# Second mixer of a diffusion backbone: input rows on all 128 partitions, copies divided anew between two engines, and the last modulation unit computed among the gated products

## The reference, cut to what matters

```python
h  = modulate(rms_norm(x, norm1_g[layer]), sh1, sc1)          # latent, 512 tokens
hc = modulate(rms_norm(ctx, norm1_g[layer]), sh1c, sc1c)      # context, 256 tokens
# s5_mixer: 64 groups of 16 channels, 64 complex states per group, two directions
for di, rev in enumerate((False, True)):
    ...
    yc_d, h_ctx = s5_scan(u_c, lam_bar, b_bar, c_mat, h0, rev, need_ctx)     # only h_ctx is used
    yl_d, _ = s5_scan(u, lam_bar, b_bar, c_mat, h_ctx, rev, True)
    y = y + yl_d
def glu(t):
    z = gelu(t)
    val, gt = jnp.split(z @ glu_w + glu_b, 2, axis=-1)
    return val * sigmoid(gt)
x = x + g1 * glu(y)
```

## Time and profile before

| | |
|---|---|
| median of 3 runs | 2510.58 us (2507.99 to 2512.06) |
| the profiled execution | 2506.16 us |
| its span | 2504.4 us, so 1.8 us lie around it |
| the mixer in it | from 1461.3 to 1760.7 us |
| busy | PE 86%, DVE 44%, ACT 20%, POOL 17% |
| mean granted PE clock | 0.952 |

### The profile page before, as it was taken

One profiled execution on the slowest core, in us unless ns is written; L12 is line 12 of the kernel. 1 busy time (PEld: TensorE's weight loads), 2 busy tenths in 40 slices (PEclk: granted clock), 3 DMA queues, 4 the chain that ended last, 5 costly groups with the idle time before them and its releaser, 6 DMA issues. The chain is left out here.

```text
span 2504.4 us, 40476 instructions
## 1 busy us (share of the span) xinstructions
PE 2143.6 (86%) x11989; PEld 1189.9 (48%) x11990; DVE 1092.3 (44%) x2311; ACT 509.8 (20%) x945; POOL 433.9 (17%) x359
## 2 busy tenths in 40 slices
PE   5889999997999999999999816699789999988874
PEld 3765444744544444444444405354444444444442
DVE  8853365944543333333333338942532222222222
ACT  3443233611121111111111125220221111100000
POOL 1000000002012222222222210000122222232332
PEclk9999999998999999999999968799799999999997
DMA  9971002003799999999999669830499999899996
GB/s 358 386 265 46 34 34 84 1 1 131 264 346 355 354 358 357 359 351 350 355 358 358 202 158 329 275 146 0 160 404 375 361 363 358 274 390 372 385 385 207
DMA packets 173622, 666.72 MB, mean 266 GB/s; under 512 B 37666, under 2 KB 48898, under 8 KB 129882
## 3 DMA queue, kind: packets, MB, share of 16 engines
q1 hardware_dynamic: 121410, 564.71, 58.7%
q0 software_dynamic: 36160, 64.84, 11.0%
q10 hardware_dynamic: 15960, 35.96, 4.1%
HBM read 617.29 MB, written 86.09 MB: 281 GB/s over the span
## 5 line engine op out<-in xcount | busy, mean ns | idle before, releaser
L1518 PE MATMUL banks_l<-slotw_l,xTw_l 128*128 128x512 f32 x800 | 358.2, 601 | 27.7 <-issue 27.7
L1529 PE MATMUL banks_l<-slotn_l,xTn_l 128*64 128x256 f32 x2816 | 325.0, 383 | 34.5 <-issue 34.5
L1529 PEld LDWEIGHTS banks_l<-slotn_l,xTn_l 128*64 128x64 f32 x2816 | 212.0, 137 | 178.9 <-issue 104.8
L1518 PEld LDWEIGHTS banks_l<-slotw_l,xTw_l 128*128 128x128 f32 x800 | 148.5, 191 | 239.3 <-issue 239.3
L1568 PE MATMUL banks_l<-slotn_l,late_l 128*64 128x512 f32 x704 | 189.9, 615 | 19.6 <-DVE late_l L1356 17.9
L1547 PE MATMUL banks_l<-slotw_l,late_l 128*128 128x512 f32 x400 | 191.8, 602 | 15.4 <-DVE late_l L1338 15.4
L977 POOL DMA_INDIRECT xgw_l<-moe_h,idxw_l x58 | 60.6, 1045 | 741.0 <-PE banks_l L1463 367.1
L1005 POOL DMA_INDIRECT moe_acc<-late_l,idxn_l x88 | 151.2, 1718 | 190.5 <-DMA moe_acc<-late_l,idxn_l 172.5
L937 POOL IOTA slotw_l<- 128x1 f32 x2 | 0.3, 140 | 729.1 <-POOLq L69 431.3
L1335 DVE TENSOR_TENSOR late_l<-late_l,banks_l 128x256 f32<-128x256 f32 x50 | 21.0, 421 | 240.2 <-ACT late_l L1107 240.2
L556 PE MATMUL ps_a<-W_a,hT_a 128*128 128x512 f32 x288 | 124.9, 595 | 0.0
(11 more groups left out here) (433 smaller groups left out, 3235.0 us busy)
## 6 DMA issues: line engine op xcount, KB each, us to landing
slotn_l<-in_exp_w_gate SPq DMA_DIRECT2D x88, 1024.0 KB
slotn_l<-in_exp_w_up SPq DMA_DIRECT2D x88, 1024.0 KB
slotn_l<-in_exp_w_down SPq DMA_DIRECT2D x88, 1024.0 KB, 12.1
slotw_l<-in_exp_w_gate SPq DMA_DIRECT2D x50, 1024.0 KB
slotw_l<-in_exp_w_up SPq DMA_DIRECT2D x50, 1024.0 KB
slotw_l<-in_exp_w_down SPq DMA_DIRECT2D x50, 1024.0 KB
w_p<-in_mod_w SPq DMA_DIRECT2D x12, 2048.0 KB, 15.4
W_a<-in_ar_w_in SPq DMA_DIRECT2D x5, 2048.0 KB, 9.4
```

Of the source, the lines that this page charges most:

```text
L1518: last = pe.matmul(pGU_w, xT_w[b % 2][:, k, :], wgu[0][b % WIDE_RING][:, :, k, :], start=(k == 0), stop=(k == KD - 1))
L1529: last = pe.matmul(pGU_n[H * side:H * side + H, b % 2], xT_n[b % 2][:, k % 4, H * (k // 4):H * (k // 4) + H], w[:, :, k, P * side:P * side ...
```

## The change

The input is laid out on all 128 partitions. Latent rows go straight into `x[:, 0:4]` (`XL`), two halves of four steps with 64 chunks each; context rows (`XC`) go four by 32, two steps each. There are six adds, six squares and six scalings where there were eight, and the eight copies to `x` are gone. ACT's queue starts with `vec`. `s5_r` is loaded by SP alone, and two of the first three modulation halves move to SP's queue, into space that is free early.

One transpose of a group becomes six products with parts of the identity: two of 64 x 64 (latent) and four of 32 x 32 (context).

The context copy of the backward direction is ACT's except for five half blocks (`DVE_CTX`), and the sweeps are no longer woven between copies. ACT also takes the backward state copies of three blocks (`ACT_BACK`).

The last late unit (two halves, two times 2 MB) is loaded once `SV` is read, into `XS`, and multiplied behind u = 1 and u = 2 of the gated products, into bank 6; the gated products rotate over three bank pairs. `gb` moves to `ZU` and is loaded last. A delay of 50 small writes on DVE before the gated products becomes 65. The final rows are written in the new order.

```diff
@@ names and layout
-        X = XS[0:NCK].rearrange("p (t d) -> p t d", t=SL)
+        XL, XC, XC1, XnC = x[:, 0:NL, :], *(XS[:, j * 2048:(j + 1) * 2048] for j in (0, 1, 1))
+        XnL = XS[:, 4096:8192].rearrange("p (g m j) -> p g m j", m=NL, j=SI)
-        gb = x[:, NL:NL + 2, :].rearrange("p t d -> p (t d)")
+        gb = ZU[:, 0, 0:2 * D]
+        DVE_CTX = (2, 5, 8, 11, 14)
+        ACT_BACK = (2, 4, 6)
+        def evicted(hb):
+            return 3 * (hb + 1) - ctx_copied(hb)
+        def ctx_copied(hb):
+            return sum(k <= hb for k in DVE_CTX)
+        def lat_rows(part, m):
+            return part.rearrange("(h m c) d -> m h c d", m=NL, h=2)[m, :, 0:NCL, :]
+        def ctx_rows(part, r):
+            return part.rearrange("(q r c) d -> r q c d", q=4, r=2)[r, :, NCL:NCK, :]
+        IN_REC = LATE - 2
+        w_glu = [XS[:, j * 4096:(j + 1) * 4096].rearrange("p (k n) -> p k n", k=HK) for j in range(2)]
@@ block.sync
-            for j in range(4):
-                sp.dma_start(X[:, 2 * j:2 * j + 2, :], parts[0].rearrange("(t c) d -> c t d", t=SL)[:, 2 * j:2 * j + 2, :])\
-                  .then_inc(x_in[j], 16)
-            for hb in range(R_ACT, NHB):
-                if hb == 4:
-                    sp.wait_ge(S['x_sum'], SL)
-                    for m in range(NL):
-                        for hh in range(2):
-                            sp.dma_start(x[hh * 64:hh * 64 + 64, m, :], X[0:64, 2 * m + hh, :]).then_inc(S['xres_in'], 16)
+            for m in range(NL):
+                sp.dma_start(XL[:, m, :], lat_rows(parts[0], m)).then_inc(x_in[m], 16)
+            for r in range(2):
+                sp.dma_start(XC[:, r, :], ctx_rows(parts[0], r)).then_inc(x_in[NL], 16)
+            for hb in range(NHB):
+                if hb == 3:
+                    sp.dma_start(w[1], mod_weights(io, *MOD_LATE[0], 1)).then_inc(m_in[1], 16)
+                if hb == 5:
+                    sp.wait_ge(S['x_sum'], NROW)
+                    sp.dma_start(w[0], mod_weights(io, *MOD_LATE[0], 0)).then_inc(m_in[0], 16)
...
-            for n in range(3, LATE):
+            for n in range(3, IN_REC):
...
-            toeplitz(LATE - 1)
-            sp.wait_ge(S['mod_mm'], LATE)
+            for b in range(IN_REC - 1, NB):
+                toeplitz(b)
+            sp.wait_ge(S['mod_mm'], IN_REC)
...
             glu_half(1)
+            sp.wait_ge(S['o_mm'], NB)
+            for n in range(IN_REC, LATE):
+                sp.dma_start(w_glu[n - IN_REC], mod_weights(io, *MOD_LATE[n // 2], n % 2)).then_inc(m_in[n % 3], 16)
+            sp.wait_ge(S['zT_mm'], NB)
+            sp.dma_start(gb, io['s5_glu_b'].to_broadcast([P, 2 * D])).then_inc(S['gb_in'], 16)
@@ block.scalar
-            act.wait_ge(S['xres_in'], 16 * 8)
-            for n in range(3):
-                act.dma_start(w[n], mod_weights(io, *MOD_LATE[n // 2], n % 2)).then_inc(m_in[n], 16)
+            act.dma_start(w[2], mod_weights(io, *MOD_LATE[1], 0)).then_inc(m_in[2], 16)
...
+                if hb not in DVE_CTX:
+                    act.activation(VH[64:P, 0:NCC, :, gs].rearrange("p c a g -> p g a c"), v_of(hb)[64:P, :, :, 0:NCC], ACT.Copy)\
+                       .then_inc(S['va_done'], 1)
...
+                if b in ACT_BACK:
+                    act.activation(SV[64:P, :, g, :], VH[64:P, NCK - 2:NCC - 2:-1, :, g].rearrange("p c a g -> p a g c"),
+                                   ACT.Copy).then_inc(S['sf_done'], 1)
@@ block.vector
-            for hb in range(NHB):
-                dve.wait_ge(S['va_done'], 2 * hb + 1)
-                dve.tensor_copy(VH[64:P, 0:NCC, :, 4 * hb:4 * hb + 4].rearrange("p c a g -> p g a c"), v_of(hb)[64:P, :, :, 0:NCC])\
-                   .then_inc(S['vd_done'], 1)
-                if 2 <= hb < 14:
-                    b, third = divmod(hb - 2, 3)
-                    sweep(b, third)
-                    if third == 2:
-                        sweep(b, 3)
-            for b in range(4, NB):
+            for b in range(NB):
+                for hb in (2 * b, 2 * b + 1):
+                    if hb in DVE_CTX:
+                        dve.wait_ge(S['va_done'], evicted(hb - 1) + 1)
...
                 for stage in range(4):
                     sweep(b, stage)
...
-            dve.wait_ge(S['mod_mm'], LATE)
+            dve.wait_ge(S['mod_mm'], IN_REC)
@@ block.tensor
-                    last = pe.transpose(ps[:, at:at + NCK], Xn[:, gg].rearrange("p t j -> p (t j)"), ident[0:NCK, 0:NCK])
+                    for h in range(2):
+                        of = slice(64 * h, 64 * h + 64)
+                        pe.matmul(ps[of, at:at + NCL], XnL[of, gg].rearrange("p m j -> p (m j)"), ident[of, of],
+                                  start=True, stop=True, skip_group_check=True)
+                    for k in range(4):
+                        of = slice(32 * k, 32 * k + 32)
+                        last = pe.matmul(ps[of, at + NCL:at + NCK], XnC[of, gg].rearrange("p r j -> p (r j)"), ident[of, of],
+                                         start=True, stop=True, skip_group_check=True)
...
-                if u >= 4:
-                    pe.wait_ge(S['out_used'], u - 3)
-                    pe.wait_ge(S['sg_pre'], u - 3)
+                if u >= 3:
+                    pe.wait_ge(S['out_used'], u - 2)
+                    pe.wait_ge(S['sg_pre'], u - 2)
...
                 last.then_inc(S['glu_mm'], 1)
+                if u in (1, 2):
+                    modulation(IN_REC + u - 1)
```

More of the change, by code:

```diff
@@ L2078, in s5_mixer @@
         S = {n: sem(n) for n in names.split()}
-        x_in = [sem(f"x_in{j}") for j in range(4)]
+        x_in = [sem(f"x_in{j}") for j in range(NL + 1)]
         r_in = [sem(f"r_in{b}") for b in range(len(Rflat))]
@@ L2184, in _ @@
             act.dma_start(vec[:, 4], io['norm1_g'][1].rearrange("(g j) -> g j", j=SI)).then_inc(S['vec_in'], 16)
+            for m in range(NL):
+                act.dma_start(XL1[:, m, :], lat_rows(parts[1], m)).then_inc(x_in[m], 16)
             act.dma_start(lam[:, 0].rearrange("p a b g -> p (a b g)"), io['s5_l8']).then_inc(S['l8_in'], 16)
[L2186 to L2190, removed]
+            for r in range(2):
+                act.dma_start(XC1[:, r, :], ctx_rows(parts[1], r)).then_inc(x_in[NL], 16)
             act.wait_ge(S['bias_zero'], 1)
@@ L2194, in _ @@
             act.activation(warm[:], ident[0:1, 0:1], ACT.Sqrt).then_inc(S['warm'], 1)
[L2195 to L2200, removed]
+            for k in range(NROW):
+                act.wait_ge(S['x_sum'], k + 1)
+                if k:
+                    act.wait_ge(S['sq_done'], k)
+                act.activation(UV[:, 0:D], XL[:, k, :] if k < NL else XC[:, k - NL, :], ACT.Square,
+                               accum_out=ss[:, k:k + 1]).then_inc(S['sq_done'], 1)
             act.wait_ge(S['var_done'], 1)
@@ L2244, in _ @@
                 for j in range(4):
[L2245 removed]
+                    act.activation(row[u % 2][32 * j:32 * j + 2, :], bank[32 * j:32 * j + 2, 0:256], ACT.Copy).then_inc(S['row_done'], 1)
                 act.wait_ge(S['row_done'], 4 * (u + 1))
@@ L2249, in _ @@
                        .then_inc(row_out[u % 2], 16)
+            for u in range(IN_REC // 2):
+                mod_row(u)
             for b in range(3):
@@ L2267, in _, with sums @@
             done = Counter(dve, S['chain'])
-            def sums(j):
-                dve.wait_ge(x_in[j], 32)
-                for s in (2 * j, 2 * j + 1):
-                    dve.tensor_tensor(X[:, s, :], X[:, s, :], X1[:, s, :], ALU.add).then_inc(S['x_sum'], 1)
+            def sums(m):
+                dve.wait_ge(x_in[m], 32 if m < NL else 64)
+                if m < NL:
+                    dve.tensor_tensor(XL[:, m, :], XL[:, m, :], XL1[:, m, :], ALU.add).then_inc(S['x_sum'], 1)
+                else:
+                    for r in range(2):
+                        dve.tensor_tensor(XC[:, r, :], XC[:, r, :], XC1[:, r, :], ALU.add).then_inc(S['x_sum'], 1)
             def squared(level):
@@ L2292, in _ @@
             dve.sem_inc(S['rep_done'], 1)
-            sums(1)
+            for m in (1, 2):
+                sums(m)
             dve.wait_ge(S['l8_in'], 16)
@@ L2419, in _ @@
                 dve.wait_ge(S['fill'], 4 * (b + 1))
-                states(b)
+                if b not in ACT_BACK:
+                    states(b)
             dve.wait_ge(S['o_mm'], NW)
@@ L2423, in _ @@
                 turned(b)
-            for _ in range(50):
+            for _ in range(65):
                 done(dve.memset(sqr[:, 0, 0, 0:1], 0.0))
```

98 lines of the change are left out of this document (54 added, 44 removed).

## The result

The changed kernel takes 2622.2 us (median of 4 runs), the kernel before beside it 2509.3: a ratio of 1.045 (95% interval 1.043 to 1.048), 113 us slower. One of the four runs took 3844.5 us at a mean granted clock of 0.59 instead of 0.93; the ratio leaves it out, and it moves the median by 0.3 us only. The profiled execution took 2621.5 us (span 2619.7 against 2504.4). The forecast was 2519, with 2530 as the upper end. Slower is right; the size is not.

What follows compares the result with a forecast made beforehand. PE was busy for 86% of the span; in the mixer, transfers, DVE, ACT or PE bound different stages. Terms -8.2 + 21.9 - 9.2 + 0 - 0.4 + 4.6 = +8.7 us gave 2519 us, range 2501 to 2530.

Steps and rivals of the forecast that it cites:

- The input: Mixer's input stage: 128 partitions load at 378 GB/s, last adds start 7.6 us earlier; 8.2 us saved in all.
- rival (c): Input: transfers do not get faster, 8 to 11 us on top, 2529; chance 0.05 shared with the late-modulation rival.
- The transposition: Mixer's transposition: six small products per group with costly shape changes make PE the limit, 36.4 us instead of 14.5, +21.9.
- Rival (a): Transposition: changes between 64 x 64 and 32 x 32 are free, total -9.2, 2501; chance 0.24 with cases near it.
- Rival (b): Transposition: clock stays at 1.2 GHz because the array waits over half of a group's time; +21, 2532; chance 0.12.
- The states: Mixer's states stage: DVE does eight sweeps and five copies instead of sixteen, 38.5 us against 47.7, a gain of 9.2.
- The recurrence: Mixer's recurrence: DVE's 42.7 us stay, some 5 us of margin before late modulation; price 0, at worst 3.
- Rival (d): Recurrence: waiting for modulation takes back the states' gain, +3 on the forecast; chance 0.05 shared with the slow-transfer rival.
- Fill and output: Mixer's fill and output: DVE drops three copies, ACT gains three and becomes the limit; gain 0.4, 2 either way.
- The gated products: Mixer's gated products: PE is full, so two half units add 4.6 us; three bank pairs cost nothing.

Runs made afterwards that it cites:

- experiment 2: Kernel before, input transfer views given a leading 4 with rows that can't be merged: 2538.3 us; with a leading 2 in the old row order: 2504.6 us.
- experiment 1: Changed kernel with each input transfer split into blocks of 64 or 32 adjacent partitions: 2536.7 us, ratio 1.011.
- experiment 7: Split changed kernel, transposition products grouped by shape, plus 80 identity products while PE waits for the normalized rows: 2516.5 us, ratio 1.003.
- experiment 8: Split changed kernel, products in the change's order, plus 108 identity products ending 1.3 us before the transposition: 2536.6 us, ratio 1.011.
- experiment 6: Split changed kernel with each round's 64 x 64 products first, then all 32 x 32 ones: 2517.9 us, ratio 1.004.
- experiment 3: Kernel before with only the copies shared anew and sweeps not woven: 2540.3 us; with 14 one-element DVE writes added: 2507.8 us.
- experiment 5: Kernel before with copies shared anew, 14 padding writes, and the last late unit moved among the gated products: 2506.5 us, ratio 0.9992.
- experiment 4: Kernel before with only the last late unit moved among the gated products, three PSUM pairs, late `gb`, longer delay: 2514.2 us, ratio 1.0020.
- experiment 9: 62 identity products before the transposition: in the kernel before 2507.3 us; with copies shared anew and the late unit moved as well, 2503.3 us.

## Why the forecast was wrong, step by step

**The input, -8.2 forecast, +85.7 measured: the step that failed.** It read "the same tensor on 128 partitions, at the kernel's end, comes at 365 to 391" and put 378 GB/s on the changed input. Two things were wrong in it. The large one is that the transfers at the kernel's end have 128 rows as their leading dimension and those of the change have 2 or 4. That set how many DMA engines take part: a share of 0.13 and 53 GB/s with 2 in front (after), 0.30 and 112 with 4 (experiment 2), 1.04 and 261 with 64 or 32 (experiment 1), worth 85 us. In the sum of the forecast nothing stood for the number of engines. The Trainium skill (DMA: Bandwidth & Descriptors, "Why a DMA increments its semaphore by 16 and not by 1") has the rule: the engines used are the largest number up to 16 that divides the slowest dimension, other than those of size 1, of both sides. The rows agree: 2 of 16 is 0.125, and 4 of 16 is 0.25, where experiment 2 has 0.26 to 0.30. I had that view in the diff and asked only for its partitions. The small one was rival (c): with all engines at work the input comes at 261 to 279 GB/s, not 378, and the stage is 40.8 us, 9 more than forecast, as the rival said (8 to 11). The forecast carried a rate over from a stage that differs in more than the partitions. At the kernel's end one queue alone loads 128 partitions in each transfer (the row with 391 also has the first transfers of the output in it, issued from 2489.0; the one with 365 is loads alone); in the split input two queues load 64 or 32 at a time. Which of these makes the difference is open. It isn't the share of engines, and it isn't the stage: weights on 128 partitions from one queue come at 410 GB/s in the last 4.6 us of experiment 1's input, at a share of 1.03.

**The transposition, +21.9 forecast, +31.3 measured: right in mechanism, the rival's clock.** The price of a group was forecast at 0.47 us at full clock and 0.70 at half; measured are 0.46 and 0.67. A change of shape was put at 0.15 and 0.19; by experiments 7 and 8 it is 0.16 at half clock ((0.67 - 0.34)/2), and 0.13 at full clock, where the grouped products need 0.20 a group in experiments 6 and 7. (The sum for the forecast's clock is 33.3 us and not 33.5, which changes nothing.) Rival (a), free changes, is out: doing 8 of them instead of 128 gives 19 us. What failed was "PE worked for 10 us before the grant was 2.4 GHz", carried over from whole-array transposes. Rival (b), the clock stays low, with 47.7 us for the stage, is what happened (45.8), and not for want of a warm start: experiment 8 gave it one, and the clock fell after 3.9 us. The profile calls PE busy for 37 of the other 40 us there. Grouped by shape, the products on 64 and 32 rows do get the high clock for a part of the stage (0.84 on average, experiment 6). Whether the clock falls for the reason that the rival gave, no run shows; it stays open.

**The states, -9.2 forecast, -7.5 measured.** Sweeps, copies and their number were as forecast. The first two half blocks were out of PSUM 7.2 us after PE began (1633.1 to 1640.4) instead of 5.8; PE's grant was 0.52 in the first 4 us of it.

**The recurrence, 0 and 0.** DVE waited for nothing, as forecast with its margin. Experiments 3 and 5 show the margin's worth: with the copies alone the wait is 4.4 us, with the unit moved too it is none. Rival (d) needed the unit to stay where it was.

**Fill and output, -0.4 and +0.2.** ACT has become the limit, and its last state copy ends 32.7 us into the stage, both as forecast.

**The gated products, +4.6 and +4.8**, and +5 by themselves in experiment 4. With three pairs PE is still busy for 114.64 of 114.70 us, so they cost nothing.

With the input's 85 us taken out, the other terms and +0.7 for the input add up to +29.6 us; the split kernel measured +28.5 by the medians.

## What to carry to other kernels

Read every DMA's view from its slowest dimension and not only by its partitions: a layout that needs `(2, 64)` or `(4, 32)` rows wants as many transfers as blocks (here that gave back 85 us), and a share of DMA time near 2/16 or 4/16 in the trace says that this was missed. A rate may be taken over from another stage only with its access pattern and with what else is in the queues. Work taken off one engine is worth something only with the wait behind it: the copies gave nothing until the late unit had gone, and together they paid for each other. And when an edit moves time in a phase that it doesn't touch, look at "issue" waits and at the packets of the instruction queues before inventing a mechanism.

## What had not been expected of the hardware

- Fourteen DVE instructions fewer, far ahead of a loop, made it wait once in each pass while instructions were loaded: 78 packets instead of 36, waits of up to 10.2 us, 32 us in all. Fourteen one-element writes undid it. The changed kernel itself has 36 packets and escaped this, by luck.
- The transfers of both queues with a 2 in front came to a share of 0.13 together, as much as two engines are worth. What one queue alone would get, no run shows.
- PE's clock fell 3.9 us into products on parts of the array that change shape two times in each 0.46 us, and stayed low for 40 us, with PE counted as busy for 37 of them (experiment 8). It held through 10.8 us of whole-array products with PE busy for 5.9 (experiment 9).
- The input on 128 partitions, loaded in blocks of 64 and 32, came only 4% faster than on 96 (261 and 251 GB/s).
